# Turned inputs loaded ahead of time, products on zeros first, and a shorter pooling product in a fused decoder layer

## The chip, the cores and the metric

The kernel runs as one program on one core of a Trainium2 chip. Its time is the device time of one execution in microseconds; the median over several runs counts. The profile is one execution taken by the hardware profiler.

## The reference, cut to what matters

One decoder layer on 256 tokens of width 1024, all float32: a token mixer with three branches, then a mixture of 32 experts of which each token uses 4.

```
xn = rmsnorm(x, g_mix)
q, k, v, u_pool, q_mem, gate_logits = split(xn @ w_in)
q, k = rotary(rmsnorm(q)), rotary(rmsnorm(k))              # 8 heads, two maps of 64
y_attn = rmsnorm(diff_attention(q, k, v)) @ w_b_attn
z[g] = trailing mean of u_pool[g] over w positions - u_pool[g]   # w = 2, 4, 8, 16
y_pool = (z[g] @ pool_w[g]) * pool_scale @ w_b_pool
kv = rmsnorm(mem, g_mem) @ w_mem_kv                        # 256 memory tokens
y_mem = cross_attention(rmsnorm(q_mem), rmsnorm(k_mem), v_mem) @ w_b_mem
h = x + (sum of sigmoid(gates) * y) @ w_out
out = h + moe(rmsnorm(h, g_ffn))                           # top 4 of 32, SwiGLU
```

## The kernel before, in words

**Mixer.** TensorE needs the inputs turned, with the 1024 channels on partitions. The weights of the mixer are cut into 22 pieces of 1024 rows by 512 columns (PIECES, L53: pool, mk, q0, mv, q1, ...), and each piece is loaded as two halves of 1 MiB. Half H = 2n + h holds the rows 512h to 512h + 511 of piece n. Five halves have a place at a time (HALVES, L62): half H + 5 goes where half H was, when TensorE has used that (half_free, L382). A unit (UNITS, L68) is the product of one piece with one tile of 128 tokens: units 0 and 1 are the pooling piece with tokens 0 to 127 and 128 to 255, units 2 and 3 are mk, 4 and 5 are q0, 6 and 7 are mv. A unit has 8 steps over the channels; the steps 0 to 3 read the first half, 4 to 7 the second.

Units 0 and 1 use halves 0 and 1 as they came, in float32 (EARLY = 2, L67). From half 2 on a half is split: ScalarE writes an upper part in a shorter format (hi, L654), VectorE the remainder (lo_whole, L914), and TensorE makes three fast products of each step in place of one slow one (L1427). Half SPLIT_AT[u] is split beside unit u: half 3 with unit 0, half 4 with unit 1, half 5 with unit 2, half 6 with unit 3, and so on. The turned inputs are split in the same way: x into XNT and memory into MEMT (upper, lower, and the plain value in the place of the lower).

The order on every engine is written out by hand. SP issues all loads of weights in one queue: x in two pieces, halves 0 and 1, memory, halves 2 and 3, small vectors and tables, half 4, the band of the pooling and its weights, then half 5, which waits for the first half of unit 1 (first_half_used), half 6 for the end of unit 1, and on. TensorE turns x by 16 transposes against an identity (L1438), does unit 0, turns memory by 16 more (L1444), and does units 1, 2, 3, 4, 5. VectorE takes each turned block out of PSUM, multiplied by the gain of its channel (gained, L930). ScalarE meanwhile squares the rows of x and of memory for the norms; GpSimd makes the inverse roots of their means (inv_ready) and then tables for the rotation (L574, eight operations), for which it waits for the constants and vectors. ScalarE takes each unit out of its PSUM bank u % 3 with the norm as a factor (evac, L631).

**Pooling.** After unit 5 the trailing means are taken by a product of U, the result of units 0 and 1, with a band matrix of 256 by 256 for each of the four groups: for each group and each tile of 128 tokens, one product with 256 columns (L1458). In row t of the band only the columns t to t + 15 differ from zero.

**Experts.** Weights of 402 MB in all stream through a ring of 9 halves of 2 MiB. The ring lies in part over the buffers of the mixer. SP issues its first loads as late units of the mixer are done (L499 to L516), and the rest as TensorE uses the ring's halves.

Of the kernel before, what the change touches and what calls it, by code (L numbers as in the profile page):

```python
# [34 lines left out]
P = 128  # L35
# [111 lines left out]

def mixer_pieces(inputs):
# [22 lines left out]
def decoder_layer(nc, x, mem, mixer_halves, b_gates, pool_w, g_ffn, w_router,  # L171
                  w_gate, b_gate, w_up, b_up, w_down, b_down, table, band, vectors, out):
    with ExitStack() as ctx:
# [77 lines left out]
        MEMT = (rows_r(4), LO_R, LO)  # L251
        V = rows(4, "t")
# [7 lines left out]
        def group_cols(u):  # L260
# [59 lines left out]
        UB = bank[0:3]  # L320


        ident_in, mem_in, con_in, gain_in, vec_in, band_in, late_in = (sem(n) for n in (
            "ident_in", "mem_in", "con_in", "gain_in", "vec_in", "band_in", "late_in"))
        x_in = [sem(f"x_in{t}") for t in range(NT)]
        raw_in = [sem(f"raw_in{i}") for i in range(HALVES)]
# [9 lines left out]
        xT_done, xT_copied, xT_high, xT_split = (sem(n) for n in ("xT_done", "xT_copied", "xT_high", "xT_split"))  # L336
        mT_done, mT_copied = sem("mT_done"), sem("mT_copied")
# [89 lines left out]
        def _(sp):  # L427
            sp.dma_start(X[:, 0, :], x[0, 0:P, :]).then_inc(x_in[0], 16)
            sp.dma_start(X[:, 1, :], x[0, P:SEQ, :]).then_inc(x_in[1], 16)
# [15 lines left out]
            sp.dma_start(con[:, P:C_ALL], table[:, P:C_ALL]).then_inc(con_in, 16)  # L445
            load(4)
# [98 lines left out]
        def _(pool):  # L545
# [8 lines left out]

            nc.gpsimd.memset(minus_half, -0.5).then_inc(exponent_ready, 1)
# [71 lines left out]
        def _(act):  # L627
            act.dma_start(con[:, C_ID:C_ID + P], table[:, C_ID:C_ID + P]).then_inc(ident_in, 16)
            act.dma_start(small[:, 0:VEC_COLS], vectors[:, 0:VEC_COLS]).then_inc(gain_in, 16)

            def evac(u, dst):  # L631

                _, name, t, _ = UNITS[u]
                n = 1 if name in ("mk", "mv") else 0
                act.wait_ge(unit_done, u + 1)
                act.wait_ge(inv_ready, n + 1)
                nc.scalar.activation(dst, UB[u % 3][:, :], ACT.Copy, scale=stat[:, 2 * n + t:2 * n + t + 1]).then_inc(bank_read[u % 3], 1)

            def square_evac(u, dst):

                _, name, t, _ = UNITS[u]
                n = 1 if name == "mk" else 0
                r = NORMED.index(u)
                act.wait_ge(unit_done, u + 1)
                act.wait_ge(inv_ready, n + 1)
                if r >= 2:
                    act.wait_ge(sq_read, r - 1)
                else:
                    act.wait_ge(squares, 4)
                nc.scalar.activation(SQ[:, r % 2, :], UB[u % 3][:, :], ACT.Square,  # L650
                                     scale=stat[:, 2 * n + t:2 * n + t + 1]).then_inc(sq_done, 1)
                evac(u, dst)
# [16 lines left out]

            for t in range(NT):  # L670
# [4 lines left out]
            for j in range(4):  # L675
                t, h = divmod(j, 2)
                at = (slice(None), slice(4 * h, 4 * h + 4), slice(t * P, (t + 1) * P))
                act.wait_ge(xT_copied, j + 1)
                nc.scalar.activation(XNT[0][at], XNT[2][at], ACT.Copy).then_inc(xT_high, 1)
            hi(2)  # L680
# [4 lines left out]
            hi_after(0)  # L685
            evac(0, U[:, 0, :])
            hi_after(1)
            evac(1, U[:, 1, :])
# [216 lines left out]
        def _(dve):  # L905
# [24 lines left out]
            def gained(n, j, place):  # L930
                t, h = divmod(j, 2)
                return nc.vector.tensor_tensor(place, bank[3 + j][:, :].rearrange("p (k n) -> p k n", k=4),
                                               gain_col[n][:, 4 * h:4 * h + 4].unsqueeze(2).to_broadcast([P, 4, P]), ALU.mult)

            def x_turned(j):
                dve.wait_ge(xT_done, j + 1)
                t, h = divmod(j, 2)
                gained(0, j, XNT[2][:, 4 * h:4 * h + 4, t * P:(t + 1) * P]).then_inc(xT_copied, 1)

            def x_lower(j):  # L940

                dve.wait_ge(xT_high, j + 1)
                t, h = divmod(j, 2)
                at = (slice(None), slice(4 * h, 4 * h + 4), slice(t * P, (t + 1) * P))
                nc.vector.tensor_tensor(XNT[1][at], XNT[2][at], XNT[0][at], ALU.subtract).then_inc(xT_split, 1)

            def mem_turned(j):
                dve.wait_ge(mT_done, j + 1)
                t, h = divmod(j, 2)
                split(lambda place: gained(1, j, place), MEMT, slice(4 * h, 4 * h + 4), slice(t * P, (t + 1) * P), mT_copied)  # L950

            dve.wait_ge(gain_in, 16)
            for j in range(4):
                x_turned(j)
            lo_whole(2)
            mem_turned(0)
            mem_turned(1)
            lo_after(0)
            mem_turned(2)
            mem_turned(3)  # L960
            dve.wait_ge(unit_done, 2)
            for j in range(4):
                x_lower(j)
# [138 lines left out]
            def add_bias(u):  # L1102
# [5 lines left out]
                nc.vector.scalar_tensor_tensor(out=g, in0=UB[u % 3][:, :], scalar=stat[:, t:t + 1], in1=g, op0=ALU.mult,  # L1108
# [9 lines left out]
            def merge(u):  # L1118
# [8 lines left out]
                nc.vector.scalar_tensor_tensor(out=dst, in0=g, scalar=1.0, in1=UB[u % 3][:, :], op0=ALU.add,  # L1127
# [82 lines left out]
            def add_h(u):  # L1210
# [4 lines left out]
                nc.vector.tensor_tensor(X[:, t, cols], UB[u % 3][:, :], X[:, t, cols], ALU.add).then_inc(h_ready, 1)  # L1215
# [171 lines left out]
        def _(pe):  # L1387
# [14 lines left out]
            def unit_k(u, first, after):  # L1402
# [5 lines left out]
                elif u >= 3:  # L1408
# [3 lines left out]
                for k in range(first, after):  # L1412
# [3 lines left out]
                    if H < EARLY:  # L1416
                        if k % 4 == 0:
                            pe.wait_ge(raw_in[H], 16)
                            pe.wait_ge(xT_copied, 2 * t + k // 4 + 1)
                        ins = nc.tensor.matmul(UB[u % 3][:, :], XNT[2][:, k, toks], raw(H)[:, cols], start=(k == 0), stop=(k == k_n - 1))  # L1420
# [5 lines left out]
                    for m, (a, b) in enumerate(((high, upper(H)), (high, lower(H)), (low, upper(H)))):  # L1426
                        ins = nc.tensor.matmul(UB[u % 3][:, :], a[:, k, toks], b[:, cols],  # L1427
# [6 lines left out]
            pe.wait_ge(ident_in, 16)  # L1434
            for j in range(4):
                t, h = divmod(j, 2)
                pe.wait_ge(x_in[t], 16)
                turn4(bank[3 + j], [X[:, t, (4 * h + b) * P:(4 * h + b + 1) * P] for b in range(4)], xT_done)  # L1438
            unit(0)
            pe.wait_ge(mem_in, 16)  # L1440
            for j in range(4):
                t, h = divmod(j, 2)
                pe.wait_ge(xT_copied, j + 1)
                turn4(bank[3 + j], [MEM[:, t, (4 * h + b) * P:(4 * h + b + 1) * P] for b in range(4)], mT_done)  # L1444
            unit(1)
            pe.wait_ge(mT_copied, 2)
            unit(2)
            pe.wait_ge(mT_copied, 4)
            unit(3)
            pe.wait_ge(xT_split, 4)  # L1450
# [355 lines left out]
```

## Time and profile before

| what | value |
|---|---|
| median of 3 runs | 1230.42 us (1228.82 to 1233.14) |
| profiled execution | 1229.14 us |
| its span in the profile | 1227.4 us |
| TensorE busy | 1158.7 us (94%) |
| VectorE, ScalarE, GpSimd busy | 446.3, 249.8, 47.8 us |
| bytes moved | 458.59 MB, mean 374 GB/s |

A busy TensorE is one with a product in flight, at whatever rate. The span is cut into 40 slices on the profile's page: in the first eight slices DMA moves 148 to 374 GB/s, and from the eleventh to the last but one 417 GB/s or more. The chain that ended last lies 68% on TensorE and 27% on DMA, and most of the DMA share is expert weights. The mixer ends by about 311 us, where the first products of the experts start.

### The profile page before, as it was taken

What the parts mean: (1) busy time and instruction counts of PE and PEld (TensorE: products, weight loads), DVE (VectorE), ACT (ScalarE), POOL (GpSimd) and SP (SyncE); (2) the same over time, 40 slices, a digit from 0 to 9 for tenths busy, and PEclk for the clock granted to TensorE, in tenths of its full rate; (3) what the DMA queues carried; (4) which work ended last, traced back from release to release, by engine and by line L of the source; (5) the groups of instructions that cost most, each with busy time, mean ns of one, the idle gap of its engine ahead of it and who ended that gap; (6) DMA issues with size and microseconds to landing.
All of it is one profiled execution on the core that took longest, in us unless ns stands there. A gap on an engine that the chain in (4) does not pass through costs nothing.

```text
span 1227.4 us, 13741 instructions
## 1 busy us (share of the span) xinstructions
PE 1158.7 (94%) x5460; PEld 586.9 (48%) x5460; DVE 446.3 (36%) x775; ACT 249.8 (20%) x409; POOL 47.8 (4%) x72
## 2 busy tenths in 40 slices
PE   8999999999999999999999899989899989899998
PEld 5888888787343443434343443434343424343433
DVE  5878798765312131231312121212222121212122
ACT  5555577632110100010010001000110000010000
POOL 2222101200000000000000000000000000000000
PEclk9999999999999999999999999999999999999999
DMA  9454545487999999999999999999999999999994
GB/s 374 148 196 171 190 154 205 169 340 312 429 417 429 428 431 428 435 431 428 437 430 428 434 434 430 430 431 434 430 430 431 434 430 429 433 428 436 430 427 204
DMA packets 28287, 458.59 MB, mean 374 GB/s; under 512 B 3232, under 2 KB 4128, under 8 KB 6624
## 3 DMA queue, kind: packets, MB, share of 16 engines
q1 hardware_dynamic: 26864, 454.14, 87.9%
q0 software_dynamic: 1104, 3.93, 1.0%
q8 instruction: 20, 0.33, 0.1%
q10 hardware_dynamic: 288, 0.10, 0.0%
q14 instruction: 11, 0.09, 0.0%
HBM read 457.11 MB, written 1.05 MB: 373 GB/s over the span
## 4 chain that ended last, share of the span: by engine, by line
PE 68%; DMA 27%; DVE 3%; ACT 1%; issue 1%; POOL 0%; SPq 0%; DVEq 0%; POOLq 0%
PE bank L1716 26%; DMA experts_ring<-in_w_up 25%; PE bank L1427 16%; PE bank L1760 11%; PE bank L1704 4%; PE bank L1644 3%; DMA back<-in_mixer_halves 2%; PE bank L1722 2%; PE bank L1391 1%; PE bank L1420 1%; PE bank L1723 1%; DVE region L1341 1%; DVE back_split L917 0%; ACT region L895 0%; ACT region L900 0%
## 5 line engine op out<-in xcount | busy, mean ns | idle before, releaser
L1716 PE MATMUL bank<-experts_ring,region 128*64 128x512 f32 x2048 | 453.4, 595 | 29.0 <-DMA experts_ring<-in_w_up 14.5
L1716 PEld LDWEIGHTS bank<-experts_ring,region 128*64 128x64 f32 x2048 | 147.9, 137 | 311.8 <-issue 290.1
L1760 PE MATMUL bank<-experts_ring,region 128*64 128x512 f32 x1024 | 226.8, 595 | 14.3 <-ACT region L895 14.3
L1427 PE MATMUL bank<-back_split,region_split 128*128 128x512 f32 x600 | 176.7, 396 | 0.1
L1760 PEld LDWEIGHTS bank<-experts_ring,region 128*64 128x64 f32 x1024 | 75.6, 137 | 143.0 <-issue 129.1
L1427 PEld LDWEIGHTS bank<-back_split,region_split 128*128 128x128 f32 x600 | 110.7, 188 | 24.5 <-issue 2.5
L1376 DVE COPY region<-bank 64x512 f32<-64x512 f32 x32 | 22.2, 694 | 227.3 <-PE bank L1760 227.3
L917 DVE TENSOR_TENSOR back_split<-back,back_split 128x2048 fp32r<-128x2048 f32 x34 | 77.9, 2292 | 32.4 <-ACT back_split L657 32.2
L1427 PE MATMUL bank<-back_split,front_split 128*128 128x512 f32 x216 | 84.4, 391 | 0.0
L1365 DVE TENSOR_SCALAR region<-bank 128x512 f32<-128x512 f32 x32 | 22.1, 691 | 161.7 <-PE bank L1723 161.7
L888 ACT ACTIVATE region<-region 128x512 f32<-128x512 f32 x32 | 20.1, 629 | 292.9 <-DVE region L1358 292.9
L1704 PE MATMUL bank<-region 128*128 128x512 f32 x128 | 61.8, 605 | 12.4 <-DVE region L1341 12.4
L657 ACT ACTIVATE back_split<-back 128x2048 fp32r<-128x2048 f32 x34 | 65.0, 1912 | 23.2 <-DMA back<-in_mixer_halves 23.2
L900 ACT ACTIVATE region<-bank 64x512 f32<-64x512 f32 x32 | 18.9, 590 | 235.4 <-PE bank L1760 235.4
L1644 PE MATMUL bank<-region 128*128 128x128 f32 x544 | 63.9, 275 | 0.9 <-DVE region L1286 0.9
L1358 DVE TENSOR_SCALAR region<-bank 128x512 f32<-128x512 f32 x32 | 22.1, 691 | 112.3 <-PE bank L1723 111.8
L1644 PEld LDWEIGHTS bank<-region 128*128 128x128 f32 x544 | 62.2, 192 | 1.0 <-DVE region L1286 1.0
L1286 DVE TENSOR_SCALAR region<-con,region,stat 128x64 f32<-128x64 f32 x68 | 16.8, 311 | 122.4 <-PE bank L1732 122.3
L1341 DVE TENSOR_TENSOR region<-bank,region 128x512 f32<-128x512 f32 x68 | 45.4, 687 | 14.2 <-PE bank L1704 12.6
L1427 PEld LDWEIGHTS bank<-back_split,front_split 128*128 128x128 f32 x216 | 40.5, 188 | 8.9
L1704 PEld LDWEIGHTS bank<-region 128*128 128x128 f32 x128 | 22.9, 188 | 42.5 <-DVE region L1341 30.4
L1391 PE MATMUL bank<-con,region 128*128 128x128 f32 x240 | 37.2, 287 | 5.4 <-DMA con<-in_table 4.5
(176 smaller groups left out, 796.2 us busy)
## 6 DMA issues: line engine op xcount, KB each, us to landing
experts_ring<-in_w_gate SPq DMA_DIRECT2D x26, 4096.0 KB, 32.5
experts_ring<-in_w_up SPq DMA_DIRECT2D x22, 4096.0 KB, 34.0
experts_ring<-in_w_down SPq DMA_DIRECT2D x20, 4096.0 KB, 35.1
experts_ring<-in_w_down SPq DMA_DIRECT2D x23, 2048.0 KB, 20.5
experts_ring<-in_w_up SPq DMA_DIRECT2D x20, 2048.0 KB, 15.8
back<-in_mixer_halves SPq DMA_DIRECT2D x36, 1024.0 KB, 4.8
experts_ring<-in_w_gate SPq DMA_DIRECT2D x12, 2048.0 KB, 12.0
front<-in_mixer_halves SPq DMA_DIRECT2D x8, 1024.0 KB, 4.9
```

Source lines behind the costliest of these rows:

```text
L657: nc.scalar.activation(upper(H), raw(H), ACT.Copy).then_inc(hi_act, 1)
L917: nc.vector.tensor_tensor(lower(H), raw(H), upper(H), ALU.subtract).then_inc(lo_ready, 1)
L1341: nc.vector.tensor_tensor(X[:, t, h * HALF:(h + 1) * HALF], bank[banks[j]][:, :], X[:, t, h * HALF:(h + 1) * HALF], ALU.add).then_inc(y_ad ...
L1358: nc.vector.tensor_scalar(GS, bank[0][:, :], LIMIT, None, ALU.min).then_inc(g_read, 1)
L1376: nc.vector.tensor_copy(OE[e * SLOTS:(e + 1) * SLOTS, HALF:D], bank[2][SLOTS:2 * SLOTS, :]).then_inc(o_hi, 1)
L1391: ins = nc.tensor.transpose(dst[:, b * P:(b + 1) * P], srcs[b], ident)
L1427: ins = nc.tensor.matmul(UB[u % 3][:, :], a[:, k, toks], b[:, cols], start=(k == 0 and m == 0), stop=(k == k_n - 1 and m == 2))
L1644: ins = nc.tensor.matmul(bank[4 + half][:, b * P:(b + 1) * P], HN[:, t, (4 * half + b) * P:(4 * half + b + 1) * P], PT[:, t, :], start=(t ...
L1704: nc.tensor.matmul(bank[6 + j % 2][:, :], PWT[:, t * P:(t + 1) * P], OE[:, h * HALF:(h + 1) * HALF], start=True, stop=True).then_inc(comb_ ...
L1716: ins = nc.tensor.matmul(dst[h * SLOTS:(h + 1) * SLOTS, :], XE[:, kk, e * SLOTS:(e + 1) * SLOTS], w[:, k, h * HALF:(h + 1) * HALF], start= ...
L1722: nc.tensor.matmul(dst[:, :], pick, BIAS_UP, start=False, stop=False)
L1760: ins = nc.tensor.matmul(bank[2][h * SLOTS:(h + 1) * SLOTS, :], AHT[:, k, half * SLOTS:(half + 1) * SLOTS], w[:, k, h * HALF:(h + 1) * HAL ...
```

## The change

1. Turned copies of x and memory are laid out in main memory ahead of the launch (turned_rows) and loaded: x in two halves of 512 KB (channels 0 to 511 and 512 to 1023, for all tokens), memory in one transfer of 1 MB. The 32 turns on TensorE go. VectorE multiplies by the gains in place, 128x1024 at a time (gained); the upper parts are ScalarE's (x_high, mem_high), the lower parts VectorE's (x_lower, mem_lower).
2. x and memory by rows are still loaded, for the norms and the residual, but behind half 3 and half 4.
3. The order on SP is now: turned x first half, half 0, turned x second half, half 1, turned memory, halves 2 and 3, x, half 4, memory, vectors, constants in one piece, band, pooling weights, half 5. The load of half 4 thus stands ahead of memory, vectors and constants.
4. GpSimd clears a tile, and TensorE makes four float32 products of 128 by 512 on it before its first unit.
5. Units 0 and 1 have banks 6 and 7 to themselves (unit_bank) and are interleaved: both first halves, then both second halves.
6. The band product reads, for the first tile of tokens, only columns 0 to 143 and, for the second, only 128 to 255. In place of the wait for the identity, TensorE waits for the constants behind the pooling product.

```
 sp:
-            sp.dma_start(X[:, 0, :], x[0, 0:P, :]).then_inc(x_in[0], 16)
-            sp.dma_start(X[:, 1, :], x[0, P:SEQ, :]).then_inc(x_in[1], 16)
+            def load_xT(h):
+                sp.dma_start(plain_x_low[:, h * 4 * SEQ:(h + 1) * 4 * SEQ], x_turned[h]).then_inc(xT_in[h], 16)
+            load_xT(0)
             load(0)
+            load_xT(1)
             load(1)
-            sp.dma_start(MEM, mem[0].rearrange("(t p) n -> p t n", p=P)).then_inc(mem_in, 16)
+            sp.dma_start(plain_mem_low, mem_turned).then_inc(mT_in, 16)
             load(2)
             load(3)
+            sp.dma_start(X[:, 0, :], x[0, 0:P, :]).then_inc(x_in[0], 16)
+            sp.dma_start(X[:, 1, :], x[0, P:SEQ, :]).then_inc(x_in[1], 16)
+            load(4)
+            sp.dma_start(MEM, mem[0].rearrange("(t p) n -> p t n", p=P)).then_inc(mem_in, 16)
 ...
-            sp.dma_start(con[:, P:C_ALL], table[:, P:C_ALL]).then_inc(con_in, 16)
-            load(4)
+            sp.dma_start(con[:, :], table).then_inc(con_in, 16)
 gpsimd:
+            nc.gpsimd.memset(probT[:, 0, :], 0.0).then_inc(cleared, 1)
 scalar:
-            act.dma_start(con[:, C_ID:C_ID + P], table[:, C_ID:C_ID + P]).then_inc(ident_in, 16)
+            x_high(0)
+            x_high(1)
+            mem_high(0)
+            hi(2)
+            hi_after(0)
+            mem_high(1)
             ... squares of x
+            hi_after(1)
+            evac(0, U[:, 0, :])
+            evac(1, U[:, 1, :])
             ... squares of memory
 vector:
+            x_gained(0)
+            x_gained(1)
+            mem_gained(0)
+            mem_gained(1)
+            mem_lower(0)
             lo_whole(2)
             lo_after(0)
+            mem_lower(1)
             dve.wait_ge(unit_done, 2)
+            x_lower(0)
+            x_lower(1)
             lo_after(1)
 tensor:
-                elif u >= 3:
+                elif u >= 5:
                     pe.wait_ge(bank_read[u % 3], u // 3)
+            pe.wait_ge(cleared, 1)
+            for _ in range(4):
+                nc.tensor.matmul(bank[5][:, :], probT[:, 0, 0:P], probT[:, 0, :], start=True, stop=True)
+            unit_k(0, 0, 4)
+            unit_k(1, 0, 4)
+            unit_k(0, 4, KD)
+            unit_k(1, 4, KD)
+            pe.wait_ge(mT_split, 1)
+            unit_k(2, 0, 4)
+            pe.wait_ge(mT_split, 2)
+            unit_k(2, 4, KD)
             unit(3)
-            pe.wait_ge(xT_split, 4)
+            pe.wait_ge(xT_split, 2)
             unit(4)
             unit(5)
 ...
-                    for t in range(NT):
-                        ins = nc.tensor.matmul(bank[4 + j][:, (g % 2) * SEQ:(g % 2 + 1) * SEQ], U[:, t, g * P:(g + 1) * P],
-                                               BAND[:, t, g, :], start=(t == 0), stop=(t == NT - 1))
+                    for t, (a, b) in enumerate(((0, P + WINDOWS[-1]), (P, SEQ))):
+                        ins = nc.tensor.matmul(bank[4 + j][:, (g % 2) * SEQ + a:(g % 2) * SEQ + b], U[:, t, g * P:(g + 1) * P],
+                                               BAND[:, t, g, a:b], start=(t == 0 and g == 2 * j), stop=(t == NT - 1),
+                                               skip_group_check=True)
                 ins.then_inc(z_done, 1)
+            pe.wait_ge(con_in, 16)
```

## Rows read from the trace of the kernel before

**Rows 1.** Windows: busy us (instructions) of PE, PEld, DVE, ACT, POOL; clock, DMA share, GB/s.
```profile
264.00:310.00 46.00, 42.96 (x238) 35.98 (x236) 27.86 (x64) 12.22 (x18) 1.67 (x4) 1.00 0.75 300
310.00:418.00 108.00, 103.65 (x488) 41.25 (x490) 27.28 (x60) 10.09 (x17) 0.00 (x0) 1.00 1.00 425
...
750.00:925.00 175.00, 160.44 (x752) 64.29 (x750) 39.83 (x72) 16.37 (x26) 0.00 (x0) 1.00 1.00 432
```

**Rows 2.** Chain that ended last, in the experts: start us, us, what.
```profile
749.39 33.96 DMA experts_ring<-in_w_up
```

**Rows 3.** Timeline of the start: start us, us, engine line op.
```profile
4.33 1.06 ACT L674 ACTIVATE region<-region 128x1024 f32<-128x1024 f32 x1 [1.39 <-DMA region<-in_x]
...
4.54 3.68 PE L1391 MATMUL bank<-con,region 128*128 128x128 f32 x16 [4.54 <-DMA con<-in_table]
...
5.93 1.31 DVE L932 TENSOR_TENSOR front<-bank,small 128x512 f32<-128x512 f32 x2 [5.93 <-DMA small<-in_vectors]
...
8.28 7.72 PE L1420 MATMUL bank<-back,front 128*128 128x512 f32 x16
...
15.84 1.91 PE L1391 MATMUL bank<-con,region 128*128 128x128 f32 x16
```

**Rows 4.** Chain that ended last, in the start and the first units.
```profile
1.64 6.60 DMA back<-in_mixer_halves
...
16.00 1.75 PE bank L1391 x16
17.75 6.87 PE bank L1420 x16
24.62 21.80 PE bank L1427 x96
46.42 3.45 PE bank L1458 x16
```

**Rows 5.** Timeline of ScalarE: the copies of halves 2, 5 and 6.
```profile
15.80 1.91 ACT L657 ACTIVATE back_split<-back 128x2048 fp32r<-128x2048 f32 x1 [6.19 <-DMA back<-in_mixer_halves]
...
28.38 1.92 ACT L657 ACTIVATE back_split<-back 128x2048 fp32r<-128x2048 f32 x1 [3.03 <-DMA back<-in_mixer_halves]
...
32.18 1.92 ACT L657 ACTIVATE back_split<-back 128x2048 fp32r<-128x2048 f32 x1 [0.73 <-DMA back<-in_mixer_halves]
```

**Rows 6.** Timeline of VectorE: half 5's subtraction, and a later wait for TensorE.
```profile
34.94 2.29 DVE L917 TENSOR_TENSOR back_split<-back,back_split 128x2048 fp32r<-128x2048 f32 x1
...
62.56 0.69 DVE L1040 TENSOR_TENSOR front<-bank,small 128x512 f32<-128x512 f32 x1 [2.38 <-PE bank L1477]
```

**Rows 7.** Timeline of the weight loads: the last with half 4, the first with half 5.
```profile
37.65 0.19 PEld L1427 LDWEIGHTS bank<-front_split 128*128 128x128 f32 x1
...
37.88 0.41 PEld L1427 LDWEIGHTS bank<-back_split,region_split 128*128 128x128 f32 x2
```

**Rows 8.** Windows of the first 24 us, columns as in rows 1.
```profile
0.00:8.00 8.00, 3.46 (x16) 3.28 (x16) 1.91 (x3) 4.63 (x7) 1.13 (x7) 1.00 0.78 300
...
8.30:15.80 7.50, 7.50 (x16) 3.39 (x17) 0.65 (x1) 1.09 (x3) 0.00 (x0) 1.00 1.02 418
17.60:24.00 6.40, 6.40 (x17) 2.84 (x16) 6.12 (x8) 6.24 (x8) 3.90 (x9) 1.00 1.03 407
```

**Rows 9.** Prices: GpSimd's clear at L612; chain at eight dispatch products of 128 columns.
```profile
L612 POOL MEMSET region<- x1: 957/957/957, 236.0 to 236.0; 128x1024 f32 x1
...
307.52 2.07 PE bank L1644 x16
```

**Rows 10.** Timeline of SP's issues; the last line begins with half 5.
```profile
8.21 2.57 SPq L448 DMA_DIRECT2D region<-in_pool_w  x1
21.22 14.68 SPq L434 DMA_DIRECT2D back<-in_mixer_halves  x4
```

**Rows 11.** Chain that ended last, up to TensorE's wait at 104.6 us.
```profile
82.47 4.78 DMA back<-in_mixer_halves
87.25 0.02 issue
87.27 1.93 ACT back_split L657
89.20 0.02 issue
89.22 2.29 DVE back_split L917
```

**Rows 12.** Timeline of GpSimd: the rotation tables.
```profile
21.02 5.45 POOL L574 TENSOR_TENSOR rot<-gqk,con 128x64 f32<-128x64 f32 x8
```

**Rows 13.** Waits of TensorE after 100 us, and the page's group of its products.
```profile
PE bank L1716 <- DMA experts_ring<-in_w_up: 14.5, 9, 1.8
...
L1716 PE MATMUL bank<-experts_ring,region 128*64 128x512 f32 x2048 | 453.4, 595 | 29.0 <-DMA experts_ring<-in_w_up 14.5
```

More of the change, by code:

```diff
@@ L145, in projection_rows, with turned_rows @@
     return np.ascontiguousarray(w.reshape(EXPERTS, KD, P, D).transpose(0, 2, 1, 3).reshape(EXPERTS, D, D))
+def turned_rows(v):
+    v = np.asarray(v)[0]
+    return v.reshape(SEQ, KD, P).transpose(2, 1, 0)
 def mixer_pieces(inputs):
@@ L171, in decoder_layer @@
 def decoder_layer(nc, x, mem, mixer_halves, b_gates, pool_w, g_ffn, w_router,
-                  w_gate, b_gate, w_up, b_up, w_down, b_down, table, band, vectors, out):
+                  w_gate, b_gate, w_up, b_up, w_down, b_down, table, band, vectors, x_turned, mem_turned, out):
     with ExitStack() as ctx:
@@ L251, in decoder_layer @@
         MEMT = (rows_r(4), LO_R, LO)
+        plain_x_low, plain_mem_low = half_slot(XLO_SLOT), half_slot(LO_SLOT)
         V = rows(4, "t")
@@ L319, in decoder_layer, with unit_bank @@
         bank = [ctx.enter_context(nc.psum_tensor(f"bank{i}", [P, HALF], F32)) for i in range(8)]
-        UB = bank[0:3]
-        ident_in, mem_in, con_in, gain_in, vec_in, band_in, late_in = (sem(n) for n in (
-            "ident_in", "mem_in", "con_in", "gain_in", "vec_in", "band_in", "late_in"))
+        def unit_bank(u):
+            return bank[6 + u] if u < 2 else bank[u % 3]
+        mem_in, con_in, gain_in, vec_in, band_in, late_in = (sem(n) for n in (
+            "mem_in", "con_in", "gain_in", "vec_in", "band_in", "late_in"))
         x_in = [sem(f"x_in{t}") for t in range(NT)]
+        xT_in = [sem(f"xT_in{h}") for h in range(2)]
+        mT_in, cleared = sem("mT_in"), sem("cleared")
         raw_in = [sem(f"raw_in{i}") for i in range(HALVES)]
@@ L335, in decoder_layer @@
         sq_done, sq_read, group_inv, h_inv = sem("sq_done"), sem("sq_read"), sem("group_inv"), sem("h_inv")
-        xT_done, xT_copied, xT_high, xT_split = (sem(n) for n in ("xT_done", "xT_copied", "xT_high", "xT_split"))
-        mT_done, mT_copied = sem("mT_done"), sem("mT_copied")
+        xT_gained, xT_high, xT_split = (sem(n) for n in ("xT_gained", "xT_high", "xT_split"))
+        mT_gained, mT_high, mT_split = (sem(n) for n in ("mT_gained", "mT_high", "mT_split"))
         unit_done = sem("unit_done")
@@ L636, in evac @@
                 act.wait_ge(inv_ready, n + 1)
-                nc.scalar.activation(dst, UB[u % 3][:, :], ACT.Copy, scale=stat[:, 2 * n + t:2 * n + t + 1]).then_inc(bank_read[u % 3], 1)
+                nc.scalar.activation(dst, unit_bank(u)[:, :], ACT.Copy, scale=stat[:, 2 * n + t:2 * n + t + 1]).then_inc(bank_read[u % 3], 1)
             def square_evac(u, dst):
@@ L668, in gate_exp, with x_high, mem_high @@
                 nc.scalar.activation(g, g, ACT.Tanh, scale=0.5).then_inc(gexp_done, 1)
+            def x_high(h):
+                act.wait_ge(xT_gained, h + 1)
+                nc.scalar.activation(XNT[0][:, 4 * h:4 * h + 4, :], XNT[2][:, 4 * h:4 * h + 4, :], ACT.Copy).then_inc(xT_high, 1)
+            def mem_high(h):
+                act.wait_ge(mT_gained, h + 1)
+                nc.scalar.activation(MEMT[0][:, 4 * h:4 * h + 4, :], MEMT[2][:, 4 * h:4 * h + 4, :], ACT.Copy).then_inc(mT_high, 1)
+            x_high(0)
[4 more added lines that the diff above has]
+            mem_high(1)
             for t in range(NT):
@@ L674, in _ @@
                 nc.scalar.activation(JUNK, X[:, t, :], ACT.Square, scale=D ** -0.5, accum_out=stat[:, t:t + 1]).then_inc(squares, 1)
[L675 to L680, printed above, removed]
+            hi_after(1)
+            evac(0, U[:, 0, :])
+            evac(1, U[:, 1, :])
             act.wait_ge(mem_in, 16)
@@ L928, in split @@
                 nc.vector.tensor_tensor(low, place, high, ALU.subtract).then_inc(signal, 1)
[L930 to L944, printed above, removed]
+            def gained(n, h, whole):
+                at = whole[:, 4 * h:4 * h + 4, :]
+                return nc.vector.tensor_tensor(at, at, gain_col[n][:, 4 * h:4 * h + 4].unsqueeze(2).to_broadcast([P, 4, SEQ]), ALU.mult)
+            def x_gained(h):
+                dve.wait_ge(xT_in[h], 16)
+                gained(0, h, XNT[2]).then_inc(xT_gained, 1)
@@ L945, in x_lower, with mem_gained, mem_lower @@
+            def mem_gained(h):
+                dve.wait_ge(mT_in, 16)
+                gained(1, h, MEMT[2]).then_inc(mT_gained, 1)
+            def x_lower(h):
+                dve.wait_ge(xT_high, h + 1)
+                at = (slice(None), slice(4 * h, 4 * h + 4), slice(None))
                 nc.vector.tensor_tensor(XNT[1][at], XNT[2][at], XNT[0][at], ALU.subtract).then_inc(xT_split, 1)
[L947 to L950, printed above, removed]
+            def mem_lower(h):
+                dve.wait_ge(mT_high, h + 1)
+                at = (slice(None), slice(4 * h, 4 * h + 4), slice(None))
+                nc.vector.tensor_tensor(MEMT[1][at], MEMT[2][at], MEMT[0][at], ALU.subtract).then_inc(mT_split, 1)
@@ L1107, in add_bias @@
                 dve.wait_ge(unit_done, u + 1)
-                nc.vector.scalar_tensor_tensor(out=g, in0=UB[u % 3][:, :], scalar=stat[:, t:t + 1], in1=g, op0=ALU.mult,
+                nc.vector.scalar_tensor_tensor(out=g, in0=unit_bank(u)[:, :], scalar=stat[:, t:t + 1], in1=g, op0=ALU.mult,
                                                op1=ALU.add).then_inc(bank_read[u % 3], 1)
@@ L1126, in merge @@
                 dst = {"p": MG[:, t, cols], "m": tmp[:, 0, :], "a": LATE_TMP}[branch]
-                nc.vector.scalar_tensor_tensor(out=dst, in0=g, scalar=1.0, in1=UB[u % 3][:, :], op0=ALU.add,
+                nc.vector.scalar_tensor_tensor(out=dst, in0=g, scalar=1.0, in1=unit_bank(u)[:, :], op0=ALU.add,
                                                op1=ALU.mult).then_inc(bank_read[u % 3], 1)
@@ L1418, in unit_k @@
                             pe.wait_ge(raw_in[H], 16)
-                            pe.wait_ge(xT_copied, 2 * t + k // 4 + 1)
-                        ins = nc.tensor.matmul(UB[u % 3][:, :], XNT[2][:, k, toks], raw(H)[:, cols], start=(k == 0), stop=(k == k_n - 1))
+                            pe.wait_ge(xT_gained, k // 4 + 1)
+                        ins = nc.tensor.matmul(unit_bank(u)[:, :], XNT[2][:, k, toks], raw(H)[:, cols], start=(k == 0), stop=(k == k_n - 1))
                         if k == 3 and t == NT - 1:
@@ L1794 @@
                 "w_down": down_rows(inputs["w_down"]), "w_gate": projection_rows(inputs["w_gate"]),
-                "w_up": projection_rows(inputs["w_up"])}
+                "w_up": projection_rows(inputs["w_up"]), "x_turned": np.ascontiguousarray(turned_rows(inputs["x"]).reshape(P, 2, 4 * SEQ).transpose(1, 0, 2)),
+                "mem_turned": turned_rows(inputs["mem"]).reshape(P, KD * SEQ)}
     arrays, args = {}, []
-    for name in _INS + ["table", "band", "vectors"]:
+    for name in _INS + ["table", "band", "vectors", "x_turned", "mem_turned"]:
         a = laid_out.get(name)
```

33 lines of the change are left out of this document (3 added, 30 removed).

## The prediction

> **What bounds the kernel now.** I read the windows first, because the kernel has two halves with different limits. From 310 us to about 1,200 us it works through the experts, and there the DMA share is 1.00 at 425 to 432 GB/s, while TensorE is busy for 160.44 of 175 us [rows 1]. In the chain of waits this half shows as long stretches of expert weights in flight [rows 2]. So the end is fixed by the moment at which the stream of expert weights begins, plus a fixed number of bytes. That moment hangs on TensorE: each of the first expert loads is issued when a late mixer unit is done. A microsecond that TensorE saves in the mixer, and still has at its end, is a microsecond at the end of the kernel; a change of the mixer is worth nothing by any other way.
>
> In the mixer the chain of waits lies on TensorE from 8.28 us on, with no gap up to 82 us: unit 0, 16 turns of memory (1.75 us), unit 1 (6.87), units 2 to 5 (21.80 in all, 5.45 each), the pooling product (3.45) [rows 3, 4]. Every stall that is near in this stretch lies between the DMA and a split: a half lands, ScalarE copies its upper part, VectorE subtracts, TensorE may use it. The one to look at is half 5 (the second half of the weights of units 4 and 5). It lands at 28.38, where ScalarE stops waiting for it [rows 5], VectorE ends its subtraction at 34.94 + 2.29 = 37.23 [rows 6], and TensorE's first product with it comes at 37.88 [rows 7]. So there is 0.65 us of slack on VectorE there, and nothing of it is left if the half lands late.
>
> **The change, part by part.**
>
> *The 32 turns go, and units 0 and 1 are interleaved.* Before, the turns of x run from 4.54 to 8.2 us, and unit 0 starts at 8.28, when half 0 has landed at 8.24 [rows 3, 4]. They lie beside the DMA and cost nothing. The turns of memory lie on the chain: 1.75 us gained [rows 4]. In their place two loads are added, 1 MiB each.
>
> *Start of unit 0.* Half 0 now has 0.5 MiB less ahead of it (one half of the turned x, not all of x). At the 418 GB/s of 8.3 to 15.8 us [rows 8] that is 0.52 MB / 418 = 1.25 us, so it lands near 7.0. The gain vectors landed at 5.93 [rows 3]; they are now ScalarE's first issue, so perhaps 5.5. The product with the gains, 128x1024, takes about half of VectorE's 2.29 us for 128x2048 [rows 6], 1.15: ready at 6.7.
>
> *The four products on zeros.* GpSimd clears 128x512 first; its 128x1024 clear takes 957 ns [rows 9], so I take 0.5 to 1, and TensorE starts at about 1.8. The trace shows that TensorE starts slow: the 16 turns of x take 3.68 us, the same 16 of memory 1.91 [rows 3]. The granted clock reads 1.00 for the whole of 0 to 8 us [rows 8], so that column does not show it; the durations do, and their ratio is that of 1.2 to 2.4 GHz. A warm product here is 6.87 / 8 = 0.86 us, a slow one 1.72; three slow and one warm end at about 7.9. They hold unit 0 back by a microsecond against its data, and give it the fast clock. Unit 0's 7.72 us then become 6.87. Four half-units of 3.43 us end at 7.9 + 13.7 = 21.6, where unit 1 ended at 24.62: **3.0 us gained at this place**. If they end at 7.0 it is 3.9, if GpSimd is late by 1 us it is 2.0. Halves 1 to 3 do not hold this up: half 1 has the same 3 MiB up to its end as before, half 2 the same 5 (15.80 [rows 5]), half 3 the same 6.
>
> *Units 2 and 3.* ScalarE: copy of half 2 from 15.8 to 17.7, of half 3 to 20.3, upper part of memory's second half to 21.4 (a 128x1024 pass of it is 1.06 [rows 3]). VectorE: lower parts of half 2 until 20.0, half 3 until 22.6, memory until 23.8. TensorE starts unit 2 at 21.6, needs the second halves at 24.3, and has them by 0.5 us. Unit 3 ends at 32.5, the first half of unit 4 at 35.2. In x_lower and half 4 (8 MiB, landing near 23.6, split by 28.4) nothing waits.
>
> *Half 5.* This is where I expect the gain to go. Its load moves sooner, since unit 1's first half is done at 14.7 and not at 21.22 [rows 10]. But all of SP's loads go through one queue, and half 5 stands behind every one. Before, 9.94 MiB up to its end (six halves, x, memory and the band 1 MiB each, 0.94 of small tables) land at 28.38. The queue is full all the while: between half 2 and half 5 it is 5.08 MB in 12.58 us, 404 GB/s, and the windows say 418 and 407 [rows 5, 8]. After, it is 11.94 MiB. The two added ones are 2.10 MB, 5.0 us at 418 and 5.2 at 404, so it lands at 33.5. Copy and subtraction follow bare, 1.93 + 2.29 and some 0.06 between them [rows 11]: TensorE may go on at **37.8, where it did at 37.88**. It stands idle from 35.2, 2.6 us. Of the 3.0 us gained 0.1 is left. Bounds: at 432 GB/s [rows 1] for these bytes 37.6; at 385 for the whole queue from half 0 on (10.85 MB in 28.2 us), 1.7 us later. The loads of x and memory in rows stand ahead of half 5 too, so their being moved gives nothing here.
>
> The Trainium skill (DMA: Bandwidth & Descriptors, Where 436 GB/s comes from) puts the ceiling of the 16 engines at 435 GB/s; the trace agrees, with 432 at most. By it, as an estimate, the two added MiB cost 4.8 us and TensorE goes on 0.2 us sooner than in my sum; no more than that can be had by better packets.
>
> *What follows half 5.* Half 6 lands 2.5 us later, at 36; ScalarE is at it at 36.7 and VectorE ends at 40.8, used from 47.7. Half 7 is subtracted last on a row of VectorE work that GpSimd's roots hold, at about 46.4; used at 50.4. GpSimd's 5.45 us of rotation tables [rows 12] now wait for memory's squares: memory by rows ends at 9 MiB, lands near 26.3, is squared by 29.5, and the tables are there by 36.5; the next root is asked for at about 38. All of it is covered. Without that cover (tables 2 us later) VectorE's norms move, and unit 6 has 4 us before it cares.
>
> *Own banks for units 0 and 1.* This takes away a wait of unit 3 for an evacuation, which is now late (ScalarE splits four halves first). The transfer costs nothing, and without it unit 3 would wait for unit 0's evacuation at 26.3.
>
> *Pooling within reach.* Eight products of 256 columns took 3.45 us, 431 ns each [rows 4]. Now four have 144 and four 128. Eight of 128 columns in the dispatch take 2.07 us [rows 9], 0.26 each at most. By columns it is 272 / 512 x 3.45 = 1.83. I take 1.95: **1.5 us gained** (1.3 to 1.6). It comes behind half 5, so it stays. The added wait for the constants (landed near 28) stands ahead of the first turn of keys and holds nothing.
>
> *Onwards.* The loads from half 9 on are issued by TensorE's units and shift with them. VectorE has 2.38 us of idle time for TensorE at 62.56, so it absorbs the 1.6 us too. The one stall by 105 us traces back to a load that TensorE itself released at 82.47 [rows 11], so it moves along.
>
> **Sum**: 0.1 + 1.5 = 1.6 us. The profiled execution took 1229.14 (span 1227.4), and would become 1227.5; it stood 1.3 below the median of the runs, 1230.42. Against that median: **1228.8 us**. A measurement of this kernel can tell about 0.3% (3.7 us) from no change, so this is "same".
>
> **Rivals.**
>
> *A. Half 5 is not late, and the whole gain stays.* Then 3.0 + 1.5 = 4.5: 1225.9 us. It needs half 5 split by 35.2, so landed by 30.9, with 12.5 MB through a queue that begins at about 2 us: 433 GB/s to the last semaphore. For it speaks that the expert stream holds 432 [rows 1]; against it the 404 to 418 at this place, with small tables in the same queue. Part of it is possible. With the upper value for the start (3.9) it would be 1225.0.
>
> *B. The clock falls in the gap before half 5.* TensorE now stands for 2.6 us, longer than any of its waits after the first. If it comes out slow, units 4 and 5 run at 1.2 GHz for a time. From the start, where slow work lasted from 4.54 to about 9.3, I take 4.8 us at half rate, a loss of 2.4: 0.8 us slower than before, 1231.2. It decides from 3.2 us of slow work on. Against it: waits of up to 1.8 us in the experts leave products at their mean of 595 ns [rows 13]. The Trainium skill (TensorE: Matmul & The Clock Gate, Part 1) says that an idle engine goes back to half rate; which side of that this gap lies, no row of before tells.
>
> *C. The queue is slower than I take it*, since more transfers of 4 KB rows stand between the halves. At 385 GB/s half 5 comes 1.7 us later and eats the pooling's gain: 1230.5.
>
> *D. Nothing of it reaches the end*, because the expert stream is bound by something that does not move. No row speaks for it: 1230.4.
>
> **How the numbers follow.** Forecast (1.0 to 2.6 us gained) 0.56; A or most of it 0.20, of which half is beyond 3.7 us once the spread of the runs (1228.82 to 1233.14) is added; C and D together 0.14; B 0.10, and little of it over 3.7 us. Range: from A's 1225.9 less 0.6 of spread, 1225.3, to B's 1231.2 and 0.3, 1231.5. Faster by over 0.3%: half of A and a little of the forecast by the spread, 0.15. Slower: 0.04. Same: 0.81.
>
> **What would show it.** Right: products on zeros from about 1.8 to 7.9, unit 1 done at 21 to 22; an idle time of TensorE of 2 to 3 us near 35, ended by the subtraction of half 5, whose copy waited for the DMA until about 33.5; 16 pooling records in about 1.95 us; the rest of the mixer as before, 1.6 us sooner, and the experts' windows at the same 430 GB/s. Wrong: no idle time near 35 (A); products of over 0.5 us behind it (B); half 5 after 35 (C); a mixer that is sooner and an end that is not (D).

## The result and the profile after

The changed kernel takes 1233.01 us (median of 20 runs, 1230.73 to 1234.39) against 1230.61 us (20 runs, 1228.29 to 1233.45): a ratio of 1.0016, 95% interval 1.0009 to 1.0023. It is 2.4 us slower. That is within 0.3% and so "same" by the bound of the prediction, but the sign is the other one, and the time lies 1.5 us outside the range. The profiled execution took 1231.81 us, its span is 1229.7.

The chain of waits of the changed kernel (start us, us, what), the stretch that answers to [rows 4] and [rows 11]:

```profile
15.93 2.29 SPq L467
18.26 16.80 DMA back<-in_mixer_halves
35.08 1.92 ACT back_split L676
37.09 2.31 DVE back_split L943
39.44 10.02 PE bank L1455 x36
49.45 1.87 PE bank L1482 x16
51.32 5.46 PE bank L1455 x24
```

Before, this stretch lay on TensorE alone. Now it goes through half 5: SP issues it at 18.26, it lands at 35.08 (28.38 in [rows 5]), it is split by 39.4, and TensorE goes on at 39.44. The first product with half 5 began at 38.10 before; the 37.88 of [rows 7] is the weight load ahead of it:

```profile
38.10 0.62 PE L1427 MATMUL bank<-back_split,region_split 128*128 128x512 f32 x2
```

That SP issues half 5 only at 18.26, and not when unit 1's first half is done, does not show as a cause of its own: the engines of the DMA are busy all the while (a share of 0.95 and more in every microsecond from 16 to 35). Two more things are in these lines. 36 products in 10.02 us are too many microseconds: 24 take 5.46, so 36 should take 8.2. And the pooling takes 1.87 in place of 3.45.

The timeline of TensorE in the changed kernel (start us, us, engine line op, and in brackets the idle time before it and what ended it) shows the gap and what follows it:

```profile
1.31 5.62 PE L1464 MATMUL bank<-probT 128*128 128x512 f32 x8 [1.31 <-POOL probT L574]
7.84 14.00 PE L1448 MATMUL bank<-back,front 128*128 128x512 f32 x32 [0.91 <-DMA back<-in_mixer_halves]
21.27 1.03 PE L1455 MATMUL bank<-back_split,region_split 128*128 128x512 f32 x2
...
35.29 0.39 PE L1455 MATMUL bank<-front_split 128*128 128x512 f32 x1
39.44 1.22 PE L1455 MATMUL bank<-back_split,region_split 128*128 128x512 f32 x2 [3.76 <-DVE back_split L943]
40.46 0.63 PE L1455 MATMUL bank<-back_split,front_split 128*128 128x512 f32 x1
40.88 1.05 PE L1455 MATMUL bank<-back_split,region_split 128*128 128x512 f32 x2
...
43.13 0.63 PE L1455 MATMUL bank<-back_split,region_split 128*128 128x512 f32 x2
```

The same kind of record is 0.39 us at 35.29 and 0.63 at 40.46; the pair is 1.05 at 40.88 and 0.63 again at 43.13. The windows of the changed kernel say why; the columns are those of [rows 1], the last three being granted clock, DMA share and GB/s:

```profile
7.80:21.30 13.50, 13.46 (x33) 6.05 (x33) 7.42 (x6) 6.31 (x6) 0.00 (x0) 1.00 1.02 424
35.60:39.40 3.80, 0.08 (x1) 0.00 (x0) 2.31 (x2) 3.80 (x4) 0.00 (x0) 0.99 1.01 420
39.40:43.10 3.70, 3.66 (x9) 2.94 (x10) 3.46 (x3) 3.50 (x4) 2.95 (x2) 0.55 0.30 124
39.40:42.80 3.40, 3.36 (x8) 2.69 (x9) 3.40 (x3) 3.40 (x4) 2.65 (x2) 0.51 0.33 135
43.10:49.30 6.20, 6.20 (x29) 5.08 (x28) 4.51 (x6) 3.07 (x3) 2.23 (x4) 1.00 0.18 58
```

TensorE was idle for 3.76 us, and came out of it at a granted clock of 0.51 (39.4 to 42.8 us), the lower of its two levels; the 0.55 of the longer window has a little of the full clock in it.

Laid side by side, the first tile of mk starts 2.8 us sooner (21.27 for 24.05); the second half of unit 4 starts 1.34 later (39.44 for 38.10); the pooling begins 3.03 later (49.45 for 46.42), which is 1.34 and another 1.69, nearly all of it slow products; and it gives 1.58 back. So unit 6 starts 1.45 us late (51.32 for 49.88). At the first products of the experts it is 2.80 (313.79 for 310.99). Most of what came to it lies in one place, a second slow spell at the dispatch, where 16 records take 3.46 us in the chain and the same 16 of the next tile 2.07. The span is 2.3 us longer. From the first product of the experts to the end of the span the twelve profiles of this document take 915.1 to 918.2 us: the end follows the mixer, but one profile alone tells it only to within some 3 us, and the medians have to carry the smaller claims.

### The profile page after: what moved, and what is told of

Same layout as the page of the kernel before. It is cut to its first block, busy times and chain, and to the rows that moved or that the text cites. A ratio compares the mean times of both kernels' runs of the same rounds, so it can differ in the third digit from the quotient of the medians.

```text
span 1229.7 us, 13682 instructions
## 1 busy us (share of the span) xinstructions
PE 1160.0 (94%) x5436; PEld 585.3 (48%) x5436; DVE 443.9 (36%) x763; ACT 251.3 (20%) x409; POOL 47.1 (4%) x73
## 3 DMA queue, kind: packets, MB, share of 16 engines
HBM read 459.21 MB, written 1.05 MB: 374 GB/s over the span
## 4 chain that ended last, share of the span: by engine, by line
PE 65%; DMA 28%; DVE 3%; ACT 1%; SPq 1%; issue 1%; POOL 0%; DVEq 0%; POOLq 0%
PE bank L1743 26%; DMA experts_ring<-in_w_up 25%; PE bank L1455 15%; PE bank L1787 11%; PE bank L1731 4%; PE bank L1671 3%; DMA back<-in_mixer_halves 2%; PE bank L1749 2%; PE bank L1419 1%; PE bank L1750 1%; DVE region L1369 1%; DVE back_split L943 1%; ACT region L921 0%; ACT region L926 0%; ACT back_split L676 0%
## 5 line engine op out<-in xcount | busy, mean ns | idle before, releaser
L921 ACT ACTIVATE region<-bank 128x512 f32<-128x512 f32 x32 | 19.1, 597 | 112.6 <-PE bank L1419 112.6
## 6 DMA issues: line engine op xcount, KB each, us to landing
experts_ring<-in_w_down SPq DMA_DIRECT2D x20, 4096.0 KB, 35.1
```

## The experiments

All are compared with the kernel before, which ran beside them on the same chip (medians 1230.26, 1230.51 and 1230.77 in the three groups of runs). The changed kernel ran in none of these groups, so a distance to it is safest between two ratios to the kernel before; its own is 1.0016.

### Without the products on zeros

```
-            pe.wait_ge(cleared, 1)
-            for _ in range(4):
-                nc.tensor.matmul(bank[5][:, :], probT[:, 0, 0:P], probT[:, 0, :], start=True, stop=True)
```

> The changed kernel without the four products on zeros. Theory (the gap costs the clock): unit 0 starts at 7.84 as now, but slow, and loses about 2 us; the first half of unit 4 ends near 37.6 in place of 35.6. Half 5 is still ready at 39.4, so the gap shrinks from 3.8 to about 1.8 us, TensorE comes out of it at full rate, and the 36 products up to the pooling take 8.2 us and not 10.0. The pooling begins near 47.7, and the kernel is about 1.7 us faster than the changed one, 1231.3 us. Rival (the slow products behind the gap come from something else, such as VectorE's and ScalarE's traffic): 10.0 us as now, no change, 1233.0.

1229.67 us (ratio 0.9989, 0.9980 to 0.9998). Taking away the part that speeds up the start makes the changed kernel 3.3 us faster, in the medians and by the ratios. Its chain:

```profile
33.85 1.93 ACT back_split L676
...
35.87 2.30 DVE back_split L943
...
38.22 8.46 PE bank L1455 x36
46.67 1.87 PE bank L1479 x16
```

TensorE waits 1.4 us for the split, not 3.8, and its clock stays at 1.00: the 36 products, with what it takes to get going, are 8.46 us. That is 1.56 of the gain. Another 1.2 is that half 5 landed at 33.85 in this execution (on that, see below), and the slow spell at the dispatch is absent too. The theory holds in its mechanism; it foresaw half of the gain.

### The gap filled with work for nothing

```
             pe.wait_ge(xT_split, 2)
-            unit(4)
+            unit_k(4, 0, 4)
+            for _ in range(4):
+                nc.tensor.matmul(bank[5][:, :], probT[:, 0, 0:P], probT[:, 0, :], start=True, stop=True)
+            unit_k(4, 4, KD)
```

> The changed kernel with four more products on zeros between the first and the second half of unit 4; they stand in the gap and do not feed the result. Theory: four take 3.4 us of the 3.8, half 5 is ready at the same time, the granted clock of 39.4 to 43.1 is 1.00 and not 0.55, and 1.7 us come back: 1231.3. Rival: same clock, same time, 1233.0. If the start of unit 5 was bound by something behind half 5, a gain in the clock would be eaten too.

1230.18 us (0.9999, 0.9991 to 1.0008): 2.8 us below the changed kernel in the medians, 2.1 by the ratios (1.0016 and 0.9999, whose intervals leave about 1.4 us on either side). Only 1.7 were expected. This is the cleanest of the runs, as half 5 lands where it did (34.99). The chain has 8.45 us for the 36 products. TensorE's timeline and the window answer to the ones above:

```profile
35.17 3.59 PE L1477 MATMUL bank<-probT 128*128 128x512 f32 x8
39.35 0.74 PE L1455 MATMUL bank<-back_split,region_split 128*128 128x512 f32 x2 [0.58 <-DVE back_split L943]
...
39.40:43.10 3.70, 3.70 (x16) 3.06 (x17) 3.37 (x3) 3.70 (x5) 3.04 (x2) 1.00 0.28 117
```

Same start at 39.35, clock 1.00, 16 records in the window for 9. So the slow products come from TensorE's idleness and from nothing that ScalarE or VectorE do. The mean granted clock over whole runs moves too: 0.9962 in the 20 runs of the changed kernel, 0.9988 in the 12 of this one, and 0.9987 in the 70 of the kernel before that stand in the three groups.

### Half 5 ahead of the band

```
+            load(5)
             sp.dma_start(BAND, band.rearrange("(t p) g n -> p t g n", p=P)).then_inc(band_in, 16)
             sp.dma_start(POOLW, pool_w.rearrange("g p n -> p g n")).then_inc(band_in, 16)
...
-            for H in range(HALVES, 2 * N0):
+            for H in range(HALVES + 1, 2 * N0):
```

> The changed kernel with half 5 loaded ahead of the band and the pooling weights (1.25 MiB). Theory (half 5 is late by the bytes ahead of it): it lands 3.1 us sooner, near 32.0, its split ends near 36.2, the gap is 0.7 us and the clock holds: 3.1 + 1.7 = 4.8 us faster than the changed kernel, 1228.2 us. The band lands near 35.5, before its use at 46. Rival (half 5 is late because SP issued it late, at 18.26, or because a share of the 16 engines lags): it lands less than 1.5 us sooner, gap over 2 us, 1231 or above.

1227.15 us (0.9964, 0.9951 to 0.9977; five runs). The same kernel ran in both later groups.

> The changed kernel with half 5 ahead of the band, once more, since it ran five times only: 1227.1 us, the pooling from 43.8, no gap of TensorE before it.

1227.16 us (0.9973, 0.9961 to 0.9984), and 1226.94 (0.9966, 0.9954 to 0.9979) the third time. ScalarE has half 5 at 30.89, without a wait, 4.2 us sooner than in the changed kernel where 3.1 were expected, and the chain has no gap behind the first product:

```profile
1.19 6.55 DMA back<-in_mixer_halves
...
7.78 14.00 PE bank L1449 x32
21.78 22.03 PE bank L1456 x96
43.81 1.87 PE bank L1483 x16
```

The pooling begins at 43.81; in the changed kernel it was 49.45, before 46.42. This is the fastest version: 3.1 to 3.8 us below the kernel before in its three groups, and some 6 below the changed one. The bytes are the same; only 1.25 MiB of them come behind half 5 and not ahead of it.

### The same, without the products on zeros

The edit is the first one on top of the third.

> The changed kernel with half 5 ahead of the band and without the products on zeros. Theory (a saving at the start is worth something only when half 5 is not late): unit 0 starts at 7.8 and slow, loses about 2.1 us, there is no later gap to absorb them, the pooling begins at 45.9 in place of 43.8, and the time is 2 us above the run with them: 1229.1. Rival (the products on zeros never matter): 1227.1.

1227.67 us (0.9977, 0.9968 to 0.9986). The pooling begins at 46.31, since the 32 records of units 0 and 1 take 16.82 us and not 14.00. But the median was only 0.5 above. I ran both again.

> Half 5 ahead of the band, no products on zeros, once more. In the profiles the pooling began 2.7 us later than with them and the experts 3.2 us later, but the medians lay only 0.5 us apart (1227.67 and 1227.16). Theory: that was the spread of few runs, and the distance is 2 us: this one 1228.9 against 1226.9. Rival: the experts give most of it back, and the distance stays at 0.5 us.

> Half 5 ahead of the band, with the products on zeros, third time: 1226.9 us by the theory, 0.5 us below the run beside it by the rival.

1228.18 (0.9978, 0.9969 to 0.9987) against 1226.94. Over all runs the means are 1228.05 (22 runs) and 1226.63 (18 runs): 1.4 us, for the 2 expected. The theory holds in sign: the products on zeros gain something here and cost 3.3 us in the changed kernel. By group the means lie 1.2 and 1.6 us apart. That the experts give back 1.3 of the 2.7 us seen at the pooling is possible; the spread of the runs leaves it open.

### The pooling alone

The kernel before with the product cut to 144 and 128 columns, as in the change.

> The kernel before with only the pooling product cut to the columns within reach. Theory: 3.45 us become 1.87, all behind stays as far apart, and the end moves by 1.6 us: 1229.0. Rival (a saving in the mixer does not reach the end): 1230.6.

1228.48 us (0.9991, 0.9982 to 1.0000), 1.8 below before, for 1.6 expected. The chain shows 1.87 us for the 16 records. So a saving in the mixer reaches the end; by this run alone the interval runs from nothing to 2.2 us, and half 5 ahead of the band makes it sure.

### Two more MiB in the kernel before

```
             load(3)
+            for i, dst in enumerate((region[2], region[9])):
+                sp.dma_start(dst[:, :], mixer_halves[i]).then_inc(extra_in, 16)
```

> The kernel before with two more loads of 1 MiB, behind half 3, into places nobody reads. Theory (the added bytes are the cost): half 5 lands 5.0 to 5.2 us later, near 33.5 in place of 28.4, its split ends near 37.8, where TensorE gets to it at 37.88: no gap, the clock holds, the pooling begins at 46.4 to 47 as now, and the time is that of before to 0 to 1 us more, 1230.3 to 1231.3. It would show that the two MiB alone cost hardly anything where TensorE is late itself. Rival (the turned loads are slow by their form): half 5 lands less than 5 us later here.

ScalarE waits for both loads before a later unit, long after they are there. 1231.47 us (1.0012, 1.0003 to 1.0021), where at most 1231.3 was expected. Half 2 lands at 15.84 as before, half 5 at 34.66: 6.3 us later for 2.10 MB, not 5.0 to 5.2.

```profile
20.68 13.96 DMA back<-in_mixer_halves
34.66 1.93 ACT back_split L660
...
36.68 2.30 DVE back_split L921
...
39.03 8.48 PE bank L1431 x36
47.50 3.45 PE bank L1462 x16
```

So the two MiB alone cost 1.1 us at the pooling, with TensorE waiting 1.1 us at full clock. It is not the turned form of the loads that is dear: plain halves cost the same.

### Half 6 held back until half 5 has landed

```
+                if H == 6:
+                    sp.wait_ge(raw_in[0], 32)
                 sp.dma_start(raw(H), half_source(H)).then_inc(raw_in[H % HALVES], 16)
```

> The changed kernel in which SP issues half 6 only when half 5 has landed. Half 5 landed 18.6 us after half 2 there and 17.9 in the run without the products on zeros; by bytes alone it should be 17.6 to 17.8. Theory A (half 6, already queued, takes a share of the engines while half 5 travels): half 5 lands 17.7 us after half 2, about 1 us sooner; half 6 lands near 39 in place of 36, before its use at 47. Time 1 us less than the changed kernel or a little more, if the shorter gap spares the clock: 1231 to 1232. Theory B (the spread is that of single executions): 18.6 as before, 1233.0, or slower if half 6 now holds unit 6.

1233.91 us (1.0024, 1.0012 to 1.0037). Half 5 lands at 34.91, 18.6 us after half 2, as in the changed kernel. That half 6 delays it has fallen. The run shows something else, since nothing is queued behind half 5. Its windows:

```profile
32.00:33.00 1.00, 1.00 (x6) 0.82 (x5) 0.00 (x0) 0.00 (x0) 1.00 (x5) 1.00 0.88 352
33.00:34.00 1.00, 1.00 (x6) 0.83 (x5) 0.00 (x0) 0.00 (x0) 1.00 (x4) 1.00 0.14 41
34.00:35.00 1.00, 1.00 (x6) 0.84 (x5) 0.00 (x0) 0.09 (x1) 0.01 (x1) 1.00 0.00 0
38.40:39.40 1.00, 0.13 (x1) 0.13 (x1) 1.00 (x2) 0.00 (x0) 0.00 (x0) 0.50 1.03 426
39.40:43.10 3.70, 3.70 (x9) 2.92 (x10) 1.80 (x2) 3.33 (x4) 1.27 (x2) 0.50 1.00 425
42.80:46.20 3.40, 3.40 (x12) 2.63 (x11) 2.40 (x3) 3.25 (x5) 1.42 (x2) 0.67 0.35 149
```

Nearly all bytes are there at 33.0, half a microsecond ahead of the 33.5 of the prediction. From 33 to 34 a share of 0.14 still works, and the landing is seen at 34.91. After the gap of 3.83 us the clock is 0.50, and 36 products take 11.16 us. Against the 8.45 of the filled gap 2.7 us are lost, where the changed kernel's profile lost 1.6. The windows tell the two apart: here the clock is down while TensorE still stands (38.4 to 39.4) and the stretch from 42.8 on has 0.67, there it has the full clock.

### What the traces say of half 5's landing

The runs leave open why half 5 is late by more than its bytes. The traces go further. They hold 16 increments of a semaphore for each load, one for each DMA engine that works on it, and ScalarE starts only behind the sixteenth (35.05 and 35.08 us in the changed kernel). Besides the program's own loads, the DMA section of the profile lists a queue of instructions: one packet of 16 KB in this part of the kernel. The windows are those of half 6 in the kernel before (28.4 to 32.2 us) and of half 5 in the changed one (32.5 to 35.1); in the kernel before the stretch from half 2 to half 5 (16 to 28.3 us) has no such line. The columns are queue and kind, packets, MB, and share of 16 engines.

```profile
q8 instruction: 1, 0.02, 1.7%
q8 instruction: 1, 0.02, 2.4%
```

All in us:

| kernel | packet of instructions starts | half 5: 1st to 15th increment | 16th |
|---|---|---|---|
| before | 29.50 | 28.02 to 28.32 | 28.35 |
| changed | 32.84 | 33.22 to 34.40 | 35.05 |
| gap filled | 32.60 | 33.23 to 34.05 | 34.97 |
| half 6 held back | 32.54 | 33.29 to 34.14 | 34.89 |
| before, two more MiB | 29.68 | 33.03 to 33.31 | 34.64 |
| no products on zeros | 34.62 | 33.22 to 33.71 | 33.83 |

The packet takes 1.02 to 1.11 us, where one of 8 KB of the weights takes 0.31. With half 6 held back it can be followed: it runs from 32.54 to 33.57; as it ends, at 33.56, a packet of weights starts that takes 0.86 us and is the last to move; and the last increment comes at 34.89. The trace does not name the engine of a packet, but the times fit one engine. Where the packet came ahead of the landing, half 5's sixteenth increment is 0.65 to 1.33 us behind the fifteenth. Where it came behind half 5, the sixteenth is at once there (0.03 and 0.12 us), and a half behind it has the late one: half 6 in the kernel before (30.82 and 32.16), and likewise in the three profiles with half 5 ahead of the band. Its start moves with TensorE: 29.5 to 29.7 in the order of before, 32.2 to 32.8 in the new order, 34.6 to 35.7 there without the products on zeros. That fits the sooner landing of half 5 in the first experiment. No run moved this packet alone, so that it is the cause is read from the order of events in the traces, and what it is worth in the kernel's time is not measured.

## Why the prediction was wrong

**Right.** The end hangs on TensorE's place in the mixer; the pooling saves 1.58 us for the 1.5 foreseen and keeps it (1.8 in the runs where it stands alone); the start in its sum (unit 1 done about 2.8 us sooner, 3.0 foreseen); that half 5 swallows this gain; that ScalarE, VectorE and GpSimd are covered elsewhere. Nothing new shows in the waits of the mixer behind half 5. The number of the start is part luck: half 0 was taken to be there at 7.0 and the products on zeros to end at 7.9, and in fact they end at 6.93 and TensorE waits 0.91 us for half 0, until 7.84. The two errors cancel. The prediction takes 432 GB/s for the most in the trace of before; that is the mean of one long window, and single slices of the profile's page reach 437.

**The step that failed first** is the landing of half 5: "it lands at 33.5", from 2.10 MB at 404 to 418 GB/s. It was 35.08, and 34.99, 34.91 and 34.66 in three experiments; only one execution had 33.85. The term was 5.1 us and measured 6.7. The part by bytes was right: the eighth of half 5's 16 increments is there at 33.47 for 28.21, 5.3 us later, and with two more MiB in the kernel before the first fifteen are there by 33.31 for 28.32, 5.0 us later. What the sum lacked is, by the traces, the sixteenth increment, which comes late where the packet of instructions comes first: 35.05 in place of 33.8, 1.2 us against the run in which the packet came later. The rows of before showed such a delay, where it cost nothing: half 6 follows half 5 by 3.8 us there (28.38 and 32.18 [rows 5]), where the prediction lets it follow by 2.5. A mean rate tells when the bytes are there on average, and a semaphore waits for the slowest share. The Trainium skill (DMA: Bandwidth & Descriptors, Why a DMA increments its semaphore by 16 and not by 1) says that up to 16 engines finish independently and only the full count means landed; the trace agrees, with fifteen increments by 34.14 us and the last at 34.89 where half 6 was held back. The increments are also further apart than before from half 2 on (15.38 to 16.51 us for 15.41 to 15.77), which is not explained. The error had a second cost, since it turned a gap of 2.6 us into one of 3.8.

**The step that failed next** is the price of that gap. The forecast gave it none, and rival B, with a chance of 0.10, 2.4 us. The filled gap gives 2.1 (by ratios) to 2.8 us (by medians) back at an unchanged landing; the profiles show 1.6 and 2.7 us lost in two executions. The runs' clocks agree: 0.0025 below before over 1,230 us is, as an estimate, 3.1 us of work at the full clock lost on the mean, the spell at the dispatch included. So B's mechanism was right and its size too, and its chance far too small. I weighed it by waits of up to 1.8 us in the experts that left the clock alone, and these said nothing of one twice as long. Rivals B and C were also taken one at a time. They are one chain: a later half makes a longer gap. B with C's landing gives 1230.5 + 2.4 = 1232.9, and 1233.01 was measured. That it meets so well is luck in part, since C's reason (a queue at 385 GB/s) was not what made half 5 late, and a second slow spell is in the profile as well. The range had no room for the pair.

**The sum as measured** at the pooling's end: 1.34 late at half 5, 1.69 lost behind it (1.57 of it slow products, by the 8.45 us of the filled gap), less 1.58: 1.45 us later than before. In the profile some 1.4 more comes with a second slow spell at the dispatch (clock 0.63 from 306 to 310 us), of which 0.9 is left in the span. It is not the change's own: of twelve profiles four have it, among them one of the three of the fastest version (0.57 from 300 to 304) and the kernel before with two more MiB, which has no gap of over 1.1 us between the start and there. Four of the others have one spell at half clock far on in the experts (0.50 from 1172 to 1175 us without the products on zeros). How often it comes at the dispatch in either kernel is not known from these profiles, so that part of the 2.4 us stays open. Rival A needed half 5 by 30.9; the third experiment put it there and gained 3.1 to 3.8 us over before, of A's 4.5. Rival D is out: that run moves the end.

## What to carry to other kernels

Before gaining time at the start, list what stands ahead of each later load in the same queue, and do not take a mean rate for the time of the last increment: here one packet of instructions went with a landing a good microsecond late. The trace of before shows such a delay at another load, and the change moves it. In this kernel 1.25 MiB in the wrong place turned a gain of 3.4 us into a loss of 2.4. Saving TensorE work ahead of a late transfer is not neutral; it lengthens the idle gap, and the gap that had grown to 3.8 us cost the clock as well, where 1.4 us did not; so removing an "improvement" or filling the gap with products for nothing can be the faster kernel. When two rivals feed each other, give the pair a chance of its own.

## What the hardware showed that was not expected

Idle times of TensorE of 1.1 and 1.4 us (two more MiB; no products on zeros) left the granted clock at 1.00, and those of 3.76 and 3.83 us were followed by 0.55 and 0.50 over the next 3.7 us; none between was seen. The slow spell behind them differed between executions, 1.6 and 2.7 us lost. A packet of 16 KB of instructions and the packet of weights behind it took 1.03 and 0.86 us (half 6 held back), and half 5, where it came ahead of its landing, had its sixteenth increment 0.65 to 1.33 us after the fifteenth. The column of the granted clock does not show the first slow spell of an execution: it reads 1.00 while the first transposes take twice as long [rows 3, 8], and shows the later ones.
